# Two sums arrays, shared out by the parity of the expert

## What is computed

```
x  = layer_norm(alpha * x + attention(x))          # alpha = 2 ** 0.25
w  = top-8 of 64 sigmoid scores per token, from 4 of 8 groups, normalised, times 2.5
y  = sum over the 8 chosen experts e of w[t, e] * ((silu(x @ Wg[e]) * (x @ Wu[e])) @ Wd[e])
y += (silu(x @ Wsg) * (x @ Wsu)) @ Wsd             # shared expert, all tokens
out = layer_norm(alpha * x + y)
```

## Time and profile before

| | |
|---|---|
| times of three runs, us | 1639.15, 1639.92, 1640.45 |
| the profiled execution: from first to last instruction, us | 1640.5 (the page gives no other time of its own for it) |
| busy, share of the span | PE 96%, PEld 80%, DVE 72%, ACT 63%, POOL 31% |
| mean granted clock of TensorE | 0.979 of 2.4 GHz |
| first additions (L682) | 63, from 787.8 to 1592.5 us |
| further additions (L692) | 30, from 804.6 to 1497.0 us |
| first to last instruction of the final stage (first pair of sums added to the end) | 1602.1 to 1640.5 us |

### The profile page before, as it was taken

The page is one execution under the profiler, slowest core; times in us unless marked ns, Lnnn a source line. Parts: engine busy times, 40 slices in busy tenths (PEclk is TensorE's granted clock), DMA queues, the critical chain, the costliest instruction groups (busy, mean ns, idle before and its releaser), DMA issues.

```text
span 1640.5 us, 32188 instructions
## 1 busy us (share of the span) xinstructions
PE 1578.0 (96%) x8246; PEld 1310.0 (80%) x8247; DVE 1182.3 (72%) x2036; ACT 1032.5 (63%) x1706; POOL 503.7 (31%) x495
## 2 busy tenths in 40 slices
PE   6999999999999999899999999999999999999986
PEld 6897888888887788778878888888888888888863
DVE  4214777777777788847777787777876787888866
ACT  3214666666666655527677787666776777877854
POOL 0000000000000135432544454543454445454426
PEclk9999999999999999899999999999999999999995
DMA  7223222222123533657999999999999999999987
GB/s 245 91 81 91 72 48 68 58 65 71 45 71 103 170 134 138 227 196 281 337 291 318 305 357 367 326 289 264 334 318 288 274 353 331 342 368 370 367 252 282
DMA packets 161320, 368.63 MB, mean 225 GB/s; under 512 B 53009, under 2 KB 73489, under 8 KB 161265
## 3 DMA queue, kind: packets, MB, share of 16 engines
q1 hardware_dynamic: 136272, 284.21, 49.7%
q0 software_dynamic: 24992, 83.73, 19.7%
HBM read 294.39 MB, written 65.11 MB: 219 GB/s over the span
## 4 chain that ended last, share of the span: by engine, by line
PE 72%; DVE 8%; DMA 8%; issue 5%; ACT 3%; ACTq 2%; POOL 1%; SPq 0%; DVEq 0%; POOLq 0%
PE bank_pair L1025 6%; PE bank_pair L1031 6%; PE bank_pair L1028 6%; DMA sums_scratch<-ys,sidx 5%; PE q_ps L91 4%; PE q_ps L93 4%; PE q_ps L92 4%; PE out_ps L916 4%; PE k_ps L894 4%; PE out_ps L1084 3%; PE out_ps L1085 3%; PE q_ps L1015 3%; PE k_ps L1052 2%; PE k_ps L1053 2%; PE k_ps L1060 2%
## 5 line engine op out<-in xcount | busy, mean ns | idle before, releaser
L1918 DVE TENSOR_TENSOR gu_lo<-raw_gu,gu_hi 128x1024 fp32r<-128x1024 f32 x260 | 306.3, 1220 | 25.5 <-ACT gu_hi L1396 25.5
L1396 ACT CAST gu_hi<-raw_gu 128x1024 fp32r<-128x1024 f32 x260 | 253.2, 1050 | 2.3 <-DMA raw_gu<-in_moe_w_gate_dram 1.5
L1025 PE MATMUL bank_pair<-gu_hi,xb_hi 128*128 128x512 f32 x576 | 233.1, 405 | 5.5 <-DVE gu_lo L1918 4.2
L1028 PE MATMUL bank_pair<-gu_lo,xb_hi 128*128 128x512 f32 x576 | 226.9, 394 | 0.0
L682 POOL DMA_INDIRECT sums_scratch<-ys,sidx x63 | 122.1, 1939 | 148.9 <-DMA sums_scratch<-ys,sidx 116.0
L1918 DVE TENSOR_TENSOR dn_lo<-raw_dn,dn_hi 128x1024 fp32r<-128x1024 f32 x130 | 152.6, 1213 | 2.9 <-ACT dn_hi L1396 2.4
L1031 PE MATMUL bank_pair<-gu_hi,xb_lo 128*128 128x512 f32 x576 | 142.7, 390 | 2.0 <-DVE xb_lo L1922 2.0
L1301 ACT CAST pt_hi<-k_ps 128x512 fp32r<-128x512 f32 (+1 forms) x192 | 85.7, 482 | 75.4 <-PE k_ps L894 74.7
L1025 PEld LDWEIGHTS bank_pair<-gu_hi,xb_hi 128*128 128x128 f32 x576 | 110.1, 191 | 28.8 <-issue 6.4
L613 POOL IOTA e<- 128x64 f32 x1 | 0.2, 185 | 428.8 <-DVE xs L1714 428.8
L1396 ACT CAST dn_hi<-raw_dn 128x1024 fp32r<-128x1024 f32 x130 | 130.0, 1052 | 2.9 <-DMA raw_dn<-in_moe_w_down_dram 2.9
(11 more groups left out here) (306 smaller groups left out, 3973.7 us busy)
## 6 DMA issues: line engine op xcount, KB each, us to landing
raw_gu<-in_moe_w_gate_dram SPq DMA_DIRECT2D x128, 512.0 KB, 6.8
raw_gu<-in_moe_w_up_dram SPq DMA_DIRECT2D x128, 512.0 KB, 8.6
raw_dn<-in_moe_w_down_dram SPq DMA_DIRECT2D x128, 512.0 KB, 8.3
wqk<-in_fox_w_in_dram SPq DMA_DIRECT2D x66, 128.0 KB, 2.5
v_scratch<-v_out SPq DMA_DIRECT2D x32, 256.0 KB, 2.8
va<-v_scratch SPq DMA_DIRECT2D x16, 512.0 KB, 4.7
fin<-sums_scratch SPq DMA_DIRECT2D x16, 512.0 KB, 8.3
xs<-in_x_dram SPq DMA_DIRECT2D x8, 512.0 KB, 7.4
```

The source lines that it names most:

```text
L1025: i = pe.matmul(o3, xb_hi[s][:, c], g_hi[:, :, c], start=c == 0, stop=False, skip_group_check=True)
L1028: pe.matmul(o3, xb_hi[s][:, c], g_lo[:, :, c], start=False, stop=False, skip_group_check=True)
L1396: a.copy(hi, raw).then_inc(S[done], 1)
L1918: dve.tensor_tensor(lo, raw, hi, ALU.subtract).then_inc(S[lo_ok], 1)
```

## The change

First additions of even experts go to `sums[0]`, of odd ones to `sums[1]`; further additions go to the other array than the first ones of their expert. A first addition no longer waits for the first addition before it (other array). It waits for the one two experts back (same array; this wait was there) and, new, for all further additions of experts before it. A further addition of expert e-1 waits, new, for the first addition of expert e-2. In the branch for experts with two or more further blocks a wait is added after its loop. At the end, `add_first` of expert 62 comes before the signal `summed` instead of after it, and SP waits for the odd experts' additions before it loads `sums[1]`, for the even ones' before `sums[0]`.

```diff
             sp.wait_ge(S["summed"], 1)
+            sp.wait_ge(sent[1], 8 * E + SENT_0[1] - 16)
             for t in range(2):
                 load_sums(1, t)
-            for i in range(2):
-                sp.wait_ge(sent[i], 8 * E + SENT_0[i] - 16 * i)
+            sp.wait_ge(sent[0], 8 * E + SENT_0[0])
             for t in range(2):
                 load_sums(0, t)
...
             def add_first(par, e):
+                before_it = earlier_of(e)
                 pool.wait_ge(sent[par], 8 * (e - par) + SENT_0[par])
                 stand(pool)
                 g.tensor_copy(sidx[par][:], tab[:, ds(e * TAB_BLOCKS, 1)]).then_inc(S["sidx_ok"], 1)
                 pool.wait_ge(S["sidx_ok"], e + 1)
-                pool.wait_ge(sent[1 - par], 8 * (e + par) + SENT_0[1 - par])
+                pool.wait_ge(sent[2], 16 * before_it + SENT_0[2])
+                stand(pool)
                 pool.wait_ge(S["scaled"], SH + e + 1)
                 stand(pool)
-                g.indirect_dma_start(out=sums[0], ...
+                g.indirect_dma_start(out=sums[par], ...
...
-            def add_further(e, k, x):
+            def add_further(par, e, k, x, firsts):
+                pool.wait_ge(sent[1 - par], firsts + SENT_0[1 - par])
+                stand(pool)
                 pool.wait_ge(sent[2], 16 * x + SENT_0[2])
...
-                g.indirect_dma_start(out=sums[1], ...
+                g.indirect_dma_start(out=sums[1 - par], ...
...
                     with pool.If(further_of(e - 1) > 0):
-                        add_further(e - 1, further_of(e - 1) - 1, xi - 1)
+                        add_further(1 - par, e - 1, further_of(e - 1) - 1, xi - 1, 8 * (e - par))
                 with pool.If(nx > 1):
                     with pool.Fori(1, nx) as k:
...
-                        add_further(e, k - 1, xi + k - 1)
+                        add_further(par, e, k - 1, xi + k - 1, 8 * (e + par) - 16)
+                    pool.wait_ge(sent[2], 16 * (xi + nx - 1) + SENT_0[2])
+                    stand(pool)
...
                 else:
+                    add_first(1 - par, e - 1)
                     if ends:
...
                         pool.sem_inc(S["summed"], 1)
-                    add_first(1 - par, e - 1)
```

More of the change, by code:

```diff
@@ L678, in add_first @@
                 pool.wait_ge(S["sidx_ok"], e + 1)
-                pool.wait_ge(sent[1 - par], 8 * (e + par) + SENT_0[1 - par])
+                pool.wait_ge(sent[2], 16 * before_it + SENT_0[2])
+                stand(pool)
                 pool.wait_ge(S["scaled"], SH + e + 1)
                 stand(pool)
-                g.indirect_dma_start(out=sums[0], out_offset=bass.IndirectOffsetOnAxis(ap=sidx[par][:, 0:1], axis=0),
+                g.indirect_dma_start(out=sums[par], out_offset=bass.IndirectOffsetOnAxis(ap=sidx[par][:, 0:1], axis=0),
                                      in_=ys[par][:], in_offset=None, compute_op=ALU.add).then_inc(sent[par], 16)
-            def add_further(e, k, x):
+            def add_further(par, e, k, x, firsts):
+                pool.wait_ge(sent[1 - par], firsts + SENT_0[1 - par])
+                stand(pool)
                 pool.wait_ge(sent[2], 16 * x + SENT_0[2])
@@ L691, in add_further @@
                 stand(pool)
-                g.indirect_dma_start(out=sums[1], out_offset=bass.IndirectOffsetOnAxis(ap=sidx[2][0:XR, 0:1], axis=0),
+                g.indirect_dma_start(out=sums[1 - par], out_offset=bass.IndirectOffsetOnAxis(ap=sidx[2][0:XR, 0:1], axis=0),
                                      in_=ys[2][0:XR], in_offset=None, compute_op=ALU.add).then_inc(sent[2], 16)
```

## The result

The changed kernel takes 1647.07 us (median of four runs, 1645.89 to 1649.31), the kernel before on the same chip 1640.18 us. The ratio is 1.0034, with a 95% interval of 1.0020 to 1.0049. A second series gave 1.0055 (1.0035 to 1.0075). The prediction was 1639.3 us, with 0.70 on no difference; the loss lies at the place that its rival C named.

What follows compares the result with a forecast made beforehand. TensorE, busy 96%, was taken as the bound, GpSimd counting only at the end. The end's -2.0 and traffic's +1.4 gave -0.6 us: profiled 1639.9, median 1639.3 us; range 1636.0 to 1642.5.

Steps and rivals of the forecast that it cites:

- rival C: The 30 further additions' wait becomes a chain, holding up `ys[2]` by 0.2 us on average: 6 us, 1645; chance 0.04.
- the new wait of a further addition: In GpSimd's list, up to 30 times, for the first addition two experts back: cost 0, uncovered up to 2.3 us each.
- First additions: Their wait for each other goes: worth nothing up to about 1490 us, taken as 0 out of 0 to 1.2 us.
- The end: Expert 62's addition goes at 1589.1 and lands at 1596.6 instead of 1598.6: gain 2.0 us.
- Rival D: Both additions stand in one queue, so nothing overlaps in effect: 1639.9 to 1641.3 us; chance 0.11.
- Traffic moved forward: Additions issued earlier make weights late in the last experts, before about 1576 us: loss 1.4 us, between 0 and 2.8.
- The prediction's price of an addition: From 1500 to 1600 us, ten additions take 28.0 us of the DMA engines, 2.8 each, as an upper bound.
- The clock: TensorE's clock in the final stage was taken to fall to 0.50 again: 0 us.
- The base: The median of the runs was put 0.6 us below the profiled execution, so 1639.92 became 1639.3 us.
- TensorE's waits before: In the expert stage a few microseconds, largest 4.6 and 4.2 us; none for a gather or an addition.

Runs made afterwards that it cites:

- e2: The kernel before, with only the new wait of a further addition for the first addition two experts back; ratio to before 1.0045.
- e1: The changed kernel, with further rows added into a third array that the output leaves out, so neither kind of addition waits for the other; ratio to before 1.0004.
- e5: The changed kernel, with further rows added into the array of their own expert's first rows; ratio to before 1.0035.
- e6: The changed kernel, with an expert's first rows added ahead of its further rows in a turn; ratio to before 1.0039.
- e4: The changed kernel, with the old wait of each first addition for the first addition before it put back; ratio to before 1.0095.
- e3: The kernel before, with only expert 62's rows sent to `sums[1]`, without waiting for expert 61's addition; ratio to before 0.9994.
- e7: As e3, and GpSimd makes the iota of the last stage after expert 62's addition is issued; ratio to before 0.9983.
- e9: The kernel of e7 run again, for a second profile and interval; ratio to before 0.9987.
- e11: The changed kernel, with two buffers for scaled further rows and the fifth count that ScalarE must read for them; ratio to before 1.0065.
- e13: The changed kernel, with ScalarE reading an unused fifth count at the start of each pair of experts; ratio to before 1.0073.
- e10: As e7, and VectorE's comparison with the iota stands behind its first two sums of the last expert's further rows; ratio to before 0.9989.

## Why the prediction was wrong

**The failed step** is "the new wait of a further addition", priced at 0. By itself it costs 0.45% (e2); in the changed kernel's two profiles 3.9 and 5.8 us are lost up to expert 57, where e1, without the waits, loses nothing. The place was right and the buffer too; two readings were not. The prediction took the 8.67 us between first addition and list copy of expert 24's further rows for the tightest pattern. The trace of before has 5.69 us at expert 2's further rows, behind an expert with none, and there the next write of `ys[2]` follows after 8.79 us; both are the smallest of their kind in that trace. By its own sum that is 9.6 - 5.7 = 3.9 us of lateness for the addition instead of 0.9, and the slack of `ys[2]` there, with the 7.1 us of landing seen after (6.1 before), is 813.38 - 804.59 - 7.1 = 1.7 us, not 2.5. So the write comes 2.2 us late; ScalarE's wait is 3.08 us, of which it spent 0.93 on TensorE before. Second, the prediction asked whether the cover holds at one place and took the thirty as alike; a minimum over the thirty places was wanted.

**Rival C** named the place and 6 us, and got 0.04. Its sign, ScalarE waiting at L1504 (L1512 after) for a further addition, is in the trace. It thought of a little loss at each of thirty experts. The profiles show a few steps; in the second one nearly all is lost at experts 3 and 4. After a step the whole pace is later, so every buffer and gather has that much more time: in the changed kernel lateness is paid in a few places, more like a maximum than like a sum. This may also be why e5 and e6 lose with their waits at different places; it is argued from the steps, not tested by itself. It is no rule: e2 and e4, with serial first additions, have new steps of 1 to 3 us as late as experts 41 and 47.

**First additions.** Right: they hardly wait for each other any more, and up to expert 57 that brings nothing (e1, -0.5). Their landing takes what it took, a median of 9.6 us (6.3 to 11.8 after, before). An expert takes mostly 9 to 18 us, so only 18 of the 62 that follow another go less than 9.6 us behind it (2 before).

**The end.** The sign was right, the size too small: 4.2 us (3.5 in the second profile) instead of 2.0. The weights were later than I had them, so expert 62's rows came when its list copy was long ready. Chain after, which answers to the earlier trace rows:

```profile
1595.31 6.53 DMA sums_scratch<-ys,sidx
1601.86 5.04 DMA fin<-sums_scratch
1606.98 2.37 POOL fin L784
```

The addition goes 0.8 us after the scaling ends (the prediction had 3.7) and lands in 6.53 us (it had 7.47); the load of the tile takes 5.04 us instead of 3.46. Rival D, no overlap in effect, is answered by e3: there expert 62's addition goes while expert 61's, issued at 1581.91, is in flight; it takes 8.96 us instead of 6.13, and from the scaling to the first sum 1.5 us are saved all the same.

```profile
1586.20 8.96 DMA sums_scratch<-ys,sidx
```

**Traffic moved forward.** The term was 1.4 us (at most 2.8); the profiles of the changed kernel show 3.5 and 7.6 us in the last five experts. But that column runs from 0.8 to 7.6 us in the seven profiles in which first additions don't wait for each other, and from -0.4 to 4.3 us in the six in which they do (means of 3.4 and 1.5); e7 and e9 are one kernel, with 2.9 and -0.1. ScalarE's waits for weights between 1480 and 1600 us tell more. After, then before (in all, times, longest):

```profile
ACT dn_hi L1404 <- DMA raw_dn<-in_moe_w_down_dram: 5.1, 4, 2.0
ACT gu_hi L1404 <- DMA raw_gu<-in_moe_w_up_dram: 4.9, 4, 2.0
ACT gu_hi L1404 <- DMA raw_gu<-in_moe_w_gate_dram: 2.3, 3, 1.2
```

```profile
ACT dn_hi L1396 <- DMA raw_dn<-in_moe_w_down_dram: 2.9, 1, 2.9
ACT gu_hi L1396 <- DMA raw_gu<-in_moe_w_gate_dram: 1.5, 1, 1.5
ACT gu_hi L1396 <- DMA raw_gu<-in_moe_w_up_dram: 0.8, 2, 0.6
```

They come to 12.3 us against 5.2; to 10.0 to 14.6 us in the two profiles of the changed kernel, e1, e5 and e6, and to 0.4 to 8.7 us in the seven profiles with serial first additions, before included. (e11 and e13, which the register load holds up, have 7.5 and 6.6.) So weights do come later when the additions are let loose: the sign was right, the 1.4 us too small in both profiles, and how much too small the scatter leaves open. The Trainium skill, page "DMA: Bandwidth & Descriptors", section "Queues, rings and completion order", has each DMA engine take turns among the queues with work; these waits agree with that in sign, and no run here shows the turns themselves. The prediction's price of an addition, 2.8 us, counts seven gathers of 128 rows; one of them has 32 rows, which makes it 2.9.

**The clock.** Priced at 0; in the profile after it held until 1612 us, and that stage became 1.1 us shorter; in the second profile it was at 0.50 from 1612, ahead of the first sum at 1614, and the stage became 0.5 us shorter.

```profile
1610.00:1612.00 2.00, 1.21 (x5) 0.76 (x5) 1.93 (x4) 1.04 (x1) 2.00 (x2) 1.00 1.04 424
1612.00:1614.00 2.00, 2.00 (x5) 1.13 (x6) 1.54 (x4) 1.78 (x4) 2.00 (x2) 0.64 1.02 412
1614.00:1616.00 2.00, 2.00 (x5) 1.16 (x4) 1.93 (x4) 1.74 (x4) 2.00 (x2) 0.50 1.04 406
```

**The base.** I set the span of the profiled run against the times of others. A run's time is 1.75 us longer than its span (1646.05 and 1644.3 in the profiled run after), so the profiled run of before was about 2.3 us slower than the median, not 0.6; the forecast, median plus shift, does not hang on it. Runs of the kernel before also scatter more than the 0.1% it was given: 1638.1 to 1646.9 us among 23 runs beside e1 to e4.

**TensorE's waits before.** The prediction's list leaves out the second largest, 4.5 us in six pieces for VectorE's split of further rows; the statement that none is for a gather or an addition holds.

```profile
PE out_ps L1084 <- DVE xo L1938: 4.5, 6, 1.0
```

## What to carry to other kernels

A wait for a landing, put into an engine's list, is a wait of all that stands behind it; price it at the tightest of all the places where it comes up, with the buffer or the gather that is next in need, and not at a typical one. A wait taken away from a list where nobody waits for that engine was worth nothing here, and much the same microseconds at another instruction of that list cost 0.34 and 0.55%. What a change is worth at the end of a kernel should be tried by itself there: here the last addition alone, with the iota moved, gave the only gain.

## What the runs showed of the hardware that was not expected

- A register load on ScalarE costs 0.6 to 0.7 us at each place where ScalarE is waited for: its idle time ahead of `ht_hi` went from 2.07 to 2.67 us with a fifth load, and the kernel was 0.2 to 0.4% slower than the changed one by it (1.0073 against 1.0034 and 1.0055; the interval overlaps that of the second). The kernel before idles 28.8 us at 14 such places.
- TensorE at 2.4 GHz instead of 1.2 for all but its last products of the final stage made the stage only 1.0 us shorter (e10); VectorE and GpSimd were busy for 3.1 to 4.0 of every 4 us there.
